# Two projections of a two-block transformer kernel change from full-precision products to rounded high and low parts

## Chip, cores and metric
The kernel runs on one core of one Trainium2 chip. The metric is device time in microseconds (us), from the start of the program to its end. The chip's engines are named as in the profile: PE is TensorE's matmul, PEld its weight load, DVE is VectorE, ACT is ScalarE, POOL is GpSimd, SP the sequencer that issues the transfers (DMA).

## What is computed
The reference runs two blocks over 256 rows of width 1024. The first block has an even and an odd layer of mixed attention; the second has a gated recurrent layer, a latent attention layer and two routed expert layers. The change touches two matrix products:

```
# odd layer of the first block: input projection, 3864 columns wide
p = rms_norm(x, l1_norm) @ l1_w_in
a, b = p[:, 0:512], p[:, 512:1024]            # a * sigmoid(b) goes into a 31-tap convolution
q, k/v, gates, memory q ... = the other columns

# recurrent block of the second
gate_in, rec_in = split(h @ w_in, 2)
gate = gelu(gate_in)
xc = causal 4-tap convolution of rec_in
r, i = sigmoid(xb @ wa + ba), sigmoid(xb @ wx + bx)
a = exp(-8 * r * softplus(-lam));  b = sqrt(1 - a*a) * (i * xc)
hs = associative_scan(a, b)
y = (gate * hs) @ w_out                        # output projection, 1024 x 1024
```

All inputs and results are float32.

## The kernel before
The program is a row of stages. In each stage every engine has its own list of instructions, written out by hand in order; an engine works through its list strictly in order, and semaphores (`wait_ge`, `then_inc`) tie the lists together. Weights come in panels of 512 columns (8 slices of 128 rows, 2 MB) into three slots; `load_panels` on SP issues a panel when the one that had the slot three panels earlier is used up (`acc_ready`).

**Two ways of multiplying.** A plain float32 matmul takes the panel as it is (lines 2171 and 2713). Some projections are computed from rounded parts instead (`project_split`, and `project_rows` with line 628): ACT rounds a slice of the weights to fp32r (the high part, line 656), DVE subtracts it from the original (the low part, the "rest", line 683), the source is split in the same way (lines 648 and 674), and PE adds three products: high by high, high by low, low by high.

**Background work on DVE.** `modulation.add(f, dve, 2)` multiplies one 512 KB tile of a modulation matrix by a row (line 358). Its tiles come into a ring of three; `modulation.load` on SP (line 347) issues tile q only when tile q - 3 is used, and each such wait stands in SP's list in front of the next panel's load.

**The odd input stage (`odd_input`).** PE turns the normed rows in eight steps (line 820), ACT and DVE store them scaled as `HT` (lines 797 and 808), and PE multiplies them with eight panels, two groups of 128 rows each; group j of panel j // 2 is copied out by ACT (line 2189). Between groups `beside(j)` puts small work on PE: after group 4 the product `a * sigmoid(b)` (line 2306) is turned (line 2094) for the convolution, after group 8 the raw keys and values are turned (line 2103), after group 11 come the compression matmuls (line 2114), and after group 15 the finished convolution is turned (line 2157). DVE's list is: its half of `HT`, 14 modulation tiles, the product, convolution taps 0 to 13 (lines 2282 and 2284), the operands of the compression (line 2317, waits for the turned raw rows), taps 14 to 16, sums of squares, taps 17 and 18, norms and rotary turns, taps 19 to 30 with more norms between them, and last the copy of the turned convolution (line 2391).

**The recurrent stage (`lru_block`).** DVE computes the states in two halves of four slices each; `hs_done` counts a half that is multiplied with its gate (line 2834). PE multiplies half 0 with both output panels, then half 1 (line 2713). Meanwhile DVE copies the gate row, runs 8 modulation tiles and the gains, and then scales and adds the four result groups (`gated`, `x_res`, lines 2876 and 2877). Then the rows are normed for the next stage, while PE runs the dummy matmuls of `keep_streaming` (line 317).

Of the kernel before, what the change touches and what calls it, by code (L numbers as in the profile page):

```python
# [97 lines left out]
def build(nc, I, out, upto=99):  # L98
# [1929 lines left out]
    load_early.append((cgain[:, :], bcast(I["l1_c_norm"])))  # L2028
    DQT = zone("d_q_t", [P, D_HEADS, S])
# [11 lines left out]
    cmp_mark = zone.at  # L2041
    RT = zone("cmp_raw_t", [P, 2, D_GROUPS, S])
    OPN = D_GROUPS * N_CMP
    OPS = zone("cmp_operand", [P, 2 * CMP_K * OPN + P - OPN])
    OP = OPS[:, 0:2 * CMP_K * OPN].rearrange("p (i k g n) -> p i k g n", i=2, k=CMP_K, g=D_GROUPS)
    RAW2 = zone("cmp_raw_twice", [P, NT, 2, D_GROUPS, 2, HD])
    room = zone("square_room", [P, 1536])
    K_SLC, K_WIN, M_Q = 2304, 2560, 3352
    dq = lambda h: DQT[:, 2 * (h % 4) + h // 4, :]

    def odd_input():
# [19 lines left out]
        turned_act, turned_dve, _, turn_ahead, turn_behind = turned_rows(odd_rows, [(HT, C("l1_norm", 0, 8), None)])  # L2071
# [5 lines left out]
        with StageBlock() as block:  # L2077
            @block.sync
            def _(sp):
                issue_early(sp)  # L2080
                modulation.load(sp, 28)
                for p in range(ps[0], ps[-1] + 1):
                    load_panels(sp, p + 3)
# [4 lines left out]
            def _(pe):  # L2088
# [72 lines left out]
                for i, p in enumerate(ps):  # L2161
                    n = ODD_PANELS[i][1]
                    w = slots[p % 3][:, 0:KD * n].rearrange("p (k n) -> p k n", k=KD)
                    wait_panel(pe, p)
                    for t in range(NT):
                        j = 2 * i + t
                        wait_acc_free(pe, group(j))
                        for k in range(KD):
                            if j == 0:
                                turn_ahead(pe, k)  # L2170
                            last = nc.tensor.matmul(acc_bank(group(j))[:, 0:n], HT[:, k, t * P:(t + 1) * P], w[:, k, :],
                                                    start=(k == 0), stop=(k == KD - 1))
                            if j == 0:
                                turn_behind(pe, k)
# [4 lines left out]
            def _(act):  # L2179
# [24 lines left out]
                turned_act(act)  # L2204
                evac(0, 1, 2, 3, 4)
# [5 lines left out]
                evac(5)  # L2211
# [37 lines left out]
                evac(14)  # L2249
                for t in range(NT):  # L2250
# [17 lines left out]
            def _(dve):  # L2268
# [52 lines left out]
                conv(14, 17)  # L2321
                dve.wait_ge(squared[0], 3)
# [71 lines left out]
            def _(pool):  # L2394
# [6 lines left out]
                for T in (DQT[:, :, :], MQT[:, :, :], PC[:, :, :, :]):  # L2401
                    f(nc.gpsimd.memset(T, 0.0))
# [4 lines left out]
                                          base=CMP_STRIDE - 1, pattern=[[CMP_STRIDE, D_HEADS]], channel_multiplier=-1), cleared_d)  # L2407

# [195 lines left out]
    LP = CONV_WIDTH - 1  # L2604
    RC = zone("rec_in_t", [P, KD, LP + S])
    GT = zone("gate_t", [P, KD, S])
    XC = zone("conv_t", [P, KD, S])
    R = zone("r_t", [P, KD, S])
    IG = zone("i_t", [P, KD, S])
# [10 lines left out]
    ONES = zone("ones", [P, P])  # L2620

    def lru_block():
# [16 lines left out]
        halves = [slice(0, KD // 2), slice(KD // 2, KD)]  # L2639
        x_done = [sem(f"lru_x_done{x}") for x in range(4)]  # L2640
# [5 lines left out]
        with StageBlock() as block:  # L2646
# [18 lines left out]
            def _(pe):  # L2665
# [37 lines left out]
                for n, half in enumerate(halves):  # L2703
                    for i in range(2):
                        w = slots[outs[i] % 3][:, 0:KD * 512].rearrange("p (k n) -> p k n", k=KD)
                        for t in range(NT):
                            g = gout + 2 * i + t
                            if n == 0:
                                wait_panel(pe, outs[i])
                                wait_acc_free(pe, g)  # L2710
                            pe.wait_ge(hs_done, n + 1)
                            for k in range(half.start, half.stop):
                                last = nc.tensor.matmul(acc_bank(g)[:, :], HS[:, k, t * P:(t + 1) * P], w[:, k, :],
                                                        start=(k == 0), stop=(k == KD - 1), skip_group_check=True)
                            if n:
                                last.then_inc(acc_ready, 1)
# [3 lines left out]
            def _(act):  # L2720
# [27 lines left out]

                turned_act(act)
# [27 lines left out]
            def _(dve):  # L2777
# [47 lines left out]

                def states(n):
# [3 lines left out]
                    for b in range(h.start, h.stop):  # L2830
                        f(v.tensor_tensor_scan(HS[:, b, :], A[:, b, :], TH[:, b, :], 0.0, ALU.mult, ALU.add),
                          wait=(b == h.stop - 1))
                    dve.wait_ge(acc_free["a"], evacuated("gel", 2 * n + 1))
                    v.tensor_tensor(HS[:, h, :], HS[:, h, :], GT[:, h, :], ALU.mult).then_inc(hs_done, 1)
# [24 lines left out]
                states(0)  # L2859
                decays(1)  # L2860
# [1260 lines left out]
```

## Time and profile before
| | |
|---|---|
| median of 3 runs | 2406.74 us (2406.36 to 2407.39) |
| profiled execution | 2404.57 us, its span 2403.3 us |
| PE busy | 2332.0 us, 97% |
| DVE busy | 1856.4 us, 77% |
| ACT busy | 1147.0 us, 48% |
| mean granted TensorE clock | 0.995 |

The span is the time from the first to the last recorded instruction; the rest of the profiled execution lies around it. Times in the rows are us from the span's start. A plain float32 matmul appears as two records. Overlapping records are normal, since the duration of one includes its way through the engine, so the pace of a stream is read from the distance of the starts.

### The profile page before, as it was taken

How to read it: one execution, taken by the hardware profiler on the slowest of the kernel's cores; microseconds unless marked ns; L12 is line 12 of the kernel's file. 1: busy time of each engine (PE TensorE's matmuls, PEld its weight loads, DVE VectorE, ACT ScalarE, POOL GpSimd, SP SyncE). 2: the span in 40 equal slices, each digit the busy share in tenths (PEclk: the TensorE clock that was granted, in tenths of full speed). 3: DMA queues.
4: the chain of work that ended last, by engine and by line, in shares of the span. 5: the costliest groups of instructions: out<-in, count | busy, mean ns of one | idle time of the engine just before them, and what ended most of it. 6: DMA issues, size and time to landing. Idle time of an engine off the chain costs nothing. (4 is left out here: it accounts for less than half of the span.)

```text
span 2403.3 us, 36868 instructions
## 1 busy us (share of the span) xinstructions
PE 2332.0 (97%) x11673; PEld 1907.2 (79%) x11673; DVE 1856.4 (77%) x4221; ACT 1147.0 (48%) x1992; POOL 177.7 (7%) x204
## 2 busy tenths in 40 slices
PE   7989999999999999999999999999999999999997
PEld 5766467868887888888888867788788888888886
DVE  5677776778997788888888855699877777777776
ACT  5674247332485544444444436317744444444443
POOL 1000000001470000000000000026400000000000
PEclk9999999999999999999999999999999999999999
DMA  6534641572214666776676641411255555555553
GB/s 250 195 113 148 239 165 36 194 270 80 91 42 165 246 254 247 258 257 249 251 258 251 253 172 71 149 52 55 90 193 190 192 192 192 192 191 187 190 189 134
DMA packets 144610, 429.28 MB, mean 179 GB/s; under 512 B 15230, under 2 KB 21374, under 8 KB 144510
## 3 DMA queue, kind: packets, MB, share of 16 engines
q1 hardware_dynamic: 144510, 428.08, 49.7%
q8 instruction: 46, 0.75, 0.1%
q14 instruction: 54, 0.44, 0.1%
HBM read 426.99 MB, written 1.05 MB: 178 GB/s over the span
## 5 line engine op out<-in xcount | busy, mean ns | idle before, releaser
L3500 PE MATMUL bank<-v_parts,weighted_high 128*128 128x512 f32 x1936 | 524.3, 392 | 0.5 <-DVE weighted_low L3646 0.5
L3486 PE MATMUL bank<-h_t_parts,u_t_high 128*128 128x512 f32 x1792 | 442.7, 389 | 0.4 <-DVE u_t_low L3621 0.4
L3500 PEld LDWEIGHTS bank<-v_parts,weighted_high 128*128 128x128 f32 x1936 | 348.1, 189 | 65.6 <-issue 2.6
L3486 PEld LDWEIGHTS bank<-h_t_parts,u_t_high 128*128 128x128 f32 x1792 | 336.3, 188 | 70.7 <-DVE u_t_low L3621 0.9
L3568 ACT ACTIVATE u_t_high<-u_ring 128x1024 fp32r<-128x1024 f32 x224 | 237.2, 1059 | 171.7 <-DMA u_ring<-in_peer_u 167.8
L3587 ACT ACTIVATE activated<-activated 128x256 f32<-128x256 f32 x224 | 93.7, 418 | 466.0 <-DVE activated L3634 466.0
L3621 DVE TENSOR_TENSOR u_t_low<-u_ring,u_t_high 128x1024 fp32r<-128x1024 f32 x224 | 273.8, 1222 | 41.2 <-ACT u_t_high L3568 33.9
L3500 PE MATMUL bank<-v_parts,weighted_low 128*128 128x512 f32 x968 | 299.0, 390 | 0.0
L3628 DVE TENSOR_TENSOR v_parts<-v_ring,v_parts 128x1024 fp32r<-128x1024 f32 x240 | 291.9, 1216 | 4.0 <-ACT v_parts L3575 4.0
L3575 ACT ACTIVATE v_parts<-v_ring 128x1024 fp32r<-128x1024 f32 x240 | 253.1, 1054 | 63.5 <-PE bank L3500 62.6
L3489 PEld LDWEIGHTS bank<-h_t_parts,u_t_low 128*128 128x128 f32 x1792 | 244.5, 190 | 17.5
L3489 PE MATMUL bank<-h_t_parts,u_t_low 128*128 128x256 f32 x1792 | 249.9, 282 | 0.0
L3634 DVE TENSOR_REDUCE activated<-bank 128x256 f32<-128x512 f32 x224 | 154.3, 689 | 83.1 <-PE bank L3489 82.2
L3500 PEld LDWEIGHTS bank<-v_parts,weighted_low 128*128 128x128 f32 x968 | 181.7, 188 | 39.7
L3644 DVE CAST weighted_high<-activated 128x256 fp32r<-128x256 f32 x242 | 71.3, 295 | 125.7 <-PE bank L3500 124.0
L3640 DVE TENSOR_TENSOR activated<-activated,gates 128x256 f32<-128x256 f32 x256 | 107.2, 419 | 10.7 <-ACT activated L3580 9.3
L3646 DVE TENSOR_TENSOR weighted_low<-activated,weighted_high 128x256 fp32r<-128x256 f32 x242 | 103.1, 426 | 8.3
L3297 POOL TENSOR_SCALAR onehot<-iota_row,slot_e,slot_gate 128x128 f32<-128x128 f32 x128 | 101.1, 791 | 52.5 <-PE bank_pair L3312 30.8
L3610 POOL TENSOR_TENSOR x_res<-x_res,gated_sum 128x512 f32<-128x512 f32 x2 | 3.3, 1641 | 1344.0 <-DVE gated_sum L3685 1344.0
L3339 ACT ACTIVATE onehot<-onehot,slot_gate 128x128 f32<-128x128 f32 x256 | 87.4, 392 | 0.1
L3273 DVE TENSOR_TENSOR onehot<-bank,slot_e 128x512 f32<-128x512 f32 x128 | 87.2, 681 | 0.0
L3656 DVE SCALAR_TENSOR_TENSOR late_tiles<-late_tiles,bank_pair 128x1024 f32<-128x1024 f32 x70 | 85.0, 1214 | 0.0
(601 smaller groups left out, 3476.5 us busy)
## 6 DMA issues: line engine op xcount, KB each, us to landing
v_ring<-in_peer_v SPq DMA_DIRECT2D x242, 512.0 KB, 3.2
u_ring<-in_peer_u SPq DMA_DIRECT2D x224, 512.0 KB, 4.5
panel<-in_l_w_in SPq DMA_DIRECT2D x15, 2048.0 KB, 8.1
late_tiles<-in_ada_w SPq DMA_DIRECT2D x54, 512.0 KB, 4.2
mod_ring<-in_ada_w SPq DMA_DIRECT2D x42, 512.0 KB, 4.6
panel<-in_peer_w_q SPq DMA_DIRECT2D x8, 2048.0 KB, 7.8
early_u<-in_peer_u SPq DMA_DIRECT2D x22, 512.0 KB, 3.3
panel<-in_l_w_out SPq DMA_DIRECT2D x4, 2560.0 KB, 8.8
```

Source lines behind the costliest of these rows:

```text
L3297: nc.gpsimd.tensor_scalar(O1[:, n % R4, POOL_TOKEN, :], iota[:, :], slot_e1[:, tok], slot_g[:, tok], ALU.is_equal, ALU.mult).then_inc(pool ...
L3486: nc.tensor.matmul(banks[2 + k][:, :], UTH[:, k, j, :], H2[:, j, :, :].rearrange("p a s -> p (a s)"), start=(j == 0), stop=False, skip_gro ...
L3489: last = nc.tensor.matmul(banks[2 + k][:, 0:S], UTL[:, k, j, :], H2[:, j, 0, :], start=False, stop=(j == KD - 1), skip_group_check=True)
L3500: last = nc.tensor.matmul(banks[4 + 2 * t + half][:, :], w[:, t * P:(t + 1) * P], v[k][:, half * 512:(half + 1) * 512], start=opens and n ...
L3568: nc.scalar.activation(UTH[:, s, :, :].rearrange("p a b -> p (a b)"), UR[:, s, :], ACT.Copy)\
L3575: nc.scalar.activation(VH[s], slot, ACT.Copy).then_inc(v_high, 1)
L3587: nc.scalar.activation(AA[:, s, :], AA[:, s, :], ACT.Gelu).then_inc(gelued, 1)
L3621: nc.vector.tensor_tensor(UTL[:, s, :, :].rearrange("p a b -> p (a b)"), UR[:, s, :], UTH[:, s, :, :].rearrange("p a b -> p (a b)").bitcas ...
L3628: nc.vector.tensor_tensor(VL[s], v_slot(b, s)[0], VH[s].bitcast(F32), ALU.subtract)\
L3634: nc.vector.tensor_reduce(AA[:, s, :], banks[2 + s][:, :].rearrange("p (a s) -> p s a", a=2), AX.X, ALU.add).then_inc(summed, 1)
L3640: nc.vector.tensor_tensor(AA[:, s, :], AA[:, s, :], g, ALU.mult).then_inc(w_full, 1)
L3646: nc.vector.tensor_tensor(low[:, :], AA[:, s, :], high[:, :].bitcast(F32), ALU.subtract)\
```

## The change
In `odd_input` the first three of eight panels, and in `lru_block` the whole output projection, are multiplied from rounded parts: ACT writes the high part into a ring (4 slices in the one place, 11 in the other), DVE writes the rest in place over the panel. In `odd_input` the source is split as well (`SRC_HIGH`, `SRC_LOW`) and still stored whole as `HT` for the other five panels. The 14 modulation tiles, which DVE had in a row, are spread: 2 within the first panel, 5 within the second, 1 within the third, 4 behind taps 0 to 13 of the convolution, 2 behind taps 14 to 16; SP's loads follow (`tiles_ahead`). The turning of `a * sigmoid(b)` moves from behind group 4 to behind slice 2 of the third panel. The clearing of `DQT` on POOL waits for the third panel. In `lru_block` the 8 last modulation tiles are put between the last 8 slices' rests.

```diff
@@ odd_input, SP
-                modulation.load(sp, 28)
+                tiles_ahead = {ps[0]: 6, ps[1]: 8, ps[3]: 4, ps[4]: 10}
                 for p in range(ps[0], ps[-1] + 1):
+                    modulation.load(sp, tiles_ahead.get(p, 0))
                     load_panels(sp, p + 3)
@@ odd_input, PE
+                for i in range(SPLIT):                       # SPLIT = 3
+                    wait_acc_free(pe, group(2 * i)); wait_acc_free(pe, group(2 * i + 1))
+                    for k in range(KD):
+                        if i == 0:
+                            pe.wait_ge(src_low, k + 1)
+                        pe.wait_ge(w_low, i * KD + k + 1)
+                        high, low = high_of(i, k), slice_in(LOW_SLOTS, i, k)
+                        for t in range(NT):
+                            for x, (lhs, w) in enumerate(((SRC_HIGH, high), (SRC_HIGH, low), (SRC_LOW, high))):
+                                last = nc.tensor.matmul(...)
+                        ...
+                        if i == 0 and k + 3 < KD:
+                            turn(k + 3)
+                        if i == 2 and k == 2:
+                            beside(4)
@@ odd_input, ACT
+                for k in range(KD):
+                    act.wait_ge(rows_turned, k + 1)
+                    nc.scalar.activation(SRC_HIGH[:, k, :], turned_bank(k), ACT.Copy, scale=norm_gain(k)).then_inc(src_high, 1)
+                    if k % 2:
+                        nc.scalar.activation(HT[:, k, :], turned_bank(k), ACT.Copy, scale=norm_gain(k)).then_inc(plain_act, 1)
+                    round_w(0, k, k + 1)
+                round_w(1, 0, 4)
+                evac(0, 1)
+                round_w(1, 4, KD)
+                round_w(2, 0, 4)
+                evac(2, 3)
+                round_w(2, 4, KD - 1)
...
+                round_w(2, KD - 1, KD)
+                evac(4, 5)
@@ odd_input, DVE
-                turned_dve(dve)
-                modulation.add(f, dve, 28)
+                for k in range(KD):
+                    ... SRC_LOW[:, k, :], and HT[:, k, :] for even k
+                    lower_w(0, k)
+                    if k in (3, 6):
+                        modulation.add(f, dve, 2)
+                for k in range(KD):
+                    lower_w(1, k)
+                    if k < 5:
+                        modulation.add(f, dve, 2)
+                for k in range(4):
+                    lower_w(2, k)
                 ... a * sigmoid(b)
+                for k in range(4, KD):
+                    lower_w(2, k)
+                    if k == 5:
+                        modulation.add(f, dve, 2)
                 dve.wait_ge(conv_in, NT)
                 conv(0, 14)
+                modulation.add(f, dve, 8)
                 ... operands
                 conv(14, 17)
+                modulation.add(f, dve, 4)
@@ lru_block, ACT
+                round_states(0)
                 gelu(2)
                 root(1)
+                round_w(0, 6)
                 gelu(3)
+                round_w(6, 8)
+                round_states(1)
+                round_w(8, len(slices))
@@ lru_block, DVE
                 mults(1)
+                lower_states(0)
                 modulation.add(f, dve, 4)
                 states(1)
+                lower_w(0, 6)
+                gated_states(1)
+                lower_w(6, 8)
+                lower_states(1)
                 ... gate row copied
-                modulation.add(f, dve, 16)
+                for s in range(8, len(slices)):
+                    lower_w(s, s + 1)
+                    modulation.add(f, dve, 2)
```

`round_w` waits until the slice that had its place in the ring is used; `lower_w` waits for the rounded slice.

## Rows read from the trace of the kernel before

**Rows 1.** Timeline of PE, odd input stage (start, duration, engine, line)

```profile
225.11 1.13 PE L2171 MATMUL bank_pair<-panel,h_t 128*128 128x512 f32 x2
...
253.79 7.03 PE L2171 MATMUL bank_pair<-panel,h_t 128*128 128x512 f32 x16
...
268.40 13.90 PE L2171 MATMUL bank<-panel,h_t 128*128 128x512 f32 x32
...
341.65 1.09 PE L2157 MATMUL bank<-ident,conv_out_t 128*128 128x128 f32 x8
```

**Rows 2.** Timeline of DVE, odd input stage (idle before, releaser in brackets)

```profile
262.47 1.38 DVE L2282 TENSOR_SCALAR conv_out_t<-conv_in_t,cols 128x256 f32<-128x256 f32 x4 [4.86 <-ACT conv_in_t L2209]
263.89 22.17 DVE L2284 SCALAR_TENSOR_TENSOR conv_out_t<-conv_in_t,cols,conv_out_t 128x256 f32<-128x256 f32 x52
291.85 4.21 DVE L2317 TENSOR_TENSOR cmp_operand<-cmp_raw_t,cmp_pos_t 64x240 f32<-64x240 f32 x8 [5.78 <-ACT cmp_raw_t L2224]
...
334.23 5.07 DVE L2284 SCALAR_TENSOR_TENSOR conv_out_t<-conv_in_t,cols,conv_out_t 128x256 f32<-128x256 f32 x12
342.34 1.29 DVE L2391 COPY conv_out<-bank 128x512 f32<-128x512 f32 x2 [3.04 <-PE bank L2157]
```

**Rows 3.** Window: odd input stage (busy of PE, PEld, DVE, ACT, POOL; clock; DMA)

```profile
225.00:342.00 117.00, 116.89 (x372) 60.83 (x373) 89.26 (x217) 32.44 (x60) 3.62 (x7) 1.00 0.62 215
```

**Rows 4.** Timeline of DVE in the recurrent stage

```profile
499.82 1.23 DVE L2829 TENSOR_TENSOR tanh_t<-tanh_t,i_t 128x1024 f32<-128x1024 f32 x1 [0.60 <-ACT tanh_t L2747]
501.08 2.44 DVE L2831 TENSOR_TENSOR_SCAN hs_t<-a_t,tanh_t 128x256 f32<-128x256 f32 x4
506.07 1.23 DVE L2834 TENSOR_TENSOR hs_t<-hs_t,gate_t 128x1024 f32<-128x1024 f32 x1 [2.55 <-ACT gate_t L2728]
507.22 1.28 DVE L2867 COPY gate_row<-bank 128x512 f32<-128x512 f32 x2
...
516.75 1.22 DVE L358 SCALAR_TENSOR_TENSOR mod_ring<-mod_ring,silu_c_row 128x1024 f32<-128x1024 f32 x1 [4.58 <-DMA mod_ring<-in_ada_w]
...
532.91 0.69 DVE L2876 TENSOR_TENSOR gated<-bank_pair,gate_row 128x512 f32<-128x512 f32 x1 [2.02 <-PE bank_pair L2713]
```

**Rows 5.** Timeline of PE from the recurrent output into the next stage

```profile
505.18 7.03 PE L2713 MATMUL bank<-panel,hs_t 128*128 128x512 f32 x16
...
532.64 5.32 PE L317 MATMUL bank<-cols,ident 128*128 128x384 f32 x16
538.42 0.85 PE L820 MATMUL bank<-ident,normed_rows 128*128 128x128 f32 x6 [0.45 <-PEq L118]
```

**Rows 6.** Timeline of PE in an output projection that already uses rounded parts

```profile
418.72 0.61 PE L628 MATMUL bank_pair<-slice_parts,src_high 128*128 128x512 f32 x2
...
419.40 0.61 PE L628 MATMUL bank_pair<-slice_parts,src_high 128*128 128x512 f32 x2
```

**Rows 7.** Groups by line, 300 to 900 us (busy, mean ns | idle before)

```profile
L683 DVE TENSOR_TENSOR slice_parts<-panel,slice_parts 128x512 fp32r<-128x512 f32 x18 | 12.3, 691 | 4.1 <-ACT slice_parts L656 4.0
...
L656 ACT ACTIVATE slice_parts<-panel 128x512 fp32r<-128x512 f32 x18 | 11.2, 628 | 4.7 <-PE bank_pair L628 3.2 <-PE bank L628 1.5
...
L674 DVE TENSOR_TENSOR src_low<-bank,src_high 128x256 fp32r<-128x256 f32 x8 | 3.4, 422 | 1.7 <-ACT src_high L648 1.7
```

**Rows 8.** SP's timeline: a panel's load in the recurrent stage

```profile
505.37 0.38 SPq L283 DMA_DIRECT2D panel<-in_peer_w_q  x1
```

**Rows 9.** The page's line on the panels' loads (KB each, median us to landing)

```profile
panel<-in_l_w_in SPq DMA_DIRECT2D x15, 2048.0 KB, 8.1
```

**Rows 10.** Windows around a gap of PE, same columns (clock third last)

```profile
150.00:152.00 2.00, 0.44 (x2) 0.20 (x2) 1.77 (x11) 1.68 (x7) 0.00 (x0) 1.00 0.88 333
152.00:154.00 2.00, 1.84 (x7) 1.43 (x8) 0.97 (x5) 1.25 (x6) 0.00 (x0) 0.69 0.05 16
154.00:156.00 2.00, 2.00 (x11) 2.00 (x10) 1.42 (x8) 1.25 (x5) 0.00 (x0) 0.50 0.00 0
156.00:158.00 2.00, 1.81 (x12) 1.29 (x10) 1.73 (x12) 1.37 (x6) 0.00 (x0) 0.96 0.00 0
```

More of the change, by code:

```diff
@@ L2041, in build @@
     cmp_mark = zone.at
+    HIGH_RING = [nc.alloc_sbuf_tensor_at(f"odd_w_high{i}", [P, 512], F32R, offset=zone.at + i * 2048) for i in range(2)]
     RT = zone("cmp_raw_t", [P, 2, D_GROUPS, S])
@@ L2620, in build @@
     ONES = zone("ones", [P, P])
+    OUT_HIGH = [zone(f"lru_out_high{i}", [P, 512], F32R) for i in range(11)]
+    OUT_LOW = [nc.alloc_sbuf_tensor_at(f"lru_out_low{i}", [P, SLOT // 4], F32R, offset=o)
+               for i, o in enumerate((PANELS, PANELS + SLOT, WORK_END - SLOT))]
     def lru_block():
@@ L2639, in lru_block, with slice_in @@
         halves = [slice(0, KD // 2), slice(KD // 2, KD)]
+        hs_high, hs_low, w_high, w_low, w_used = (sem(f"lru_{x}") for x in ("hs_high", "hs_low", "w_high", "w_low", "w_used"))
+        slices = [(n, i, k) for n in range(2) for i in range(2) for k in range(halves[n].start, halves[n].stop)]
+        def slice_in(tiles, s):
+            _, i, k = slices[s]
+            return tiles[outs[i] % 3][:, k * 512:(k + 1) * 512]
         x_done = [sem(f"lru_x_done{x}") for x in range(4)]
@@ L2702, in _ @@
                                              start=True, stop=True).then_inc(row_ready, 1)
[L2703 to L2716, printed above, removed]
+                for s, (n, i, k) in enumerate(slices):
+                    if n == 0 and k == 0:
+                        wait_acc_free(pe, gout + 2 * i)
+                        wait_acc_free(pe, gout + 2 * i + 1)
+                    if i == 0 and k == halves[n].start:
+                        pe.wait_ge(hs_low, n + 1)
+                    pe.wait_ge(w_low, s + 1)
+                    high, low = OUT_HIGH[s % 11][:, :], slice_in(OUT_LOW, s)
+                    for t in range(NT):
+                        for x, (lhs, w) in enumerate(((HS_HIGH, high), (HS_HIGH, low), (HS_LOW, high))):
+                            last = nc.tensor.matmul(acc_bank(gout + 2 * i + t)[:, :], lhs[:, k, t * P:(t + 1) * P], w,
+                                                    start=(k == 0 and x == 0), stop=(k == KD - 1 and x == 2),
+                                                    skip_group_check=True)
+                        if k == KD - 1:
+                            last.then_inc(acc_ready, 1)
+                    if k < KD - 1:
+                        last.then_inc(w_used, 1)
                 keep_streaming(banks[7], 8)
@@ L2747, in root, with round_w, round_states @@
                     nc.scalar.activation(TH[:, halves[n], :], TH[:, halves[n], :], ACT.Sqrt, scale=-1.0).then_inc(root_ready, 1)
+                def round_w(lo, hi):
+                    for s in range(lo, hi):
+                        wait_panel(act, outs[slices[s][1]])
+                        if s >= 11:
+                            act.wait_ge(w_used, s - 10)
+                        nc.scalar.activation(OUT_HIGH[s % 11][:, :], slice_in(slots, s), ACT.Copy).then_inc(w_high, 1)
+                def round_states(n):
+                    act.wait_ge(hs_done, n + 1)
+                    nc.scalar.activation(HS_HIGH[:, halves[n], :], HS[:, halves[n], :], ACT.Copy).then_inc(hs_high, 1)
                 turned_act(act)
@@ L2859, in _ @@
                 states(0)
+                gated_states(0)
                 decays(1)
```

94 lines of the change are left out of this document (82 added, 12 removed).

## The prediction
> **What bounds the kernel now.** I read the page first: PE is busy for 97% of the span, and the changed places are two short stretches of it. A share over the whole span says nothing about them, so I went to the timelines by engine and looked for the wait that ends last in each.
>
> In the odd input stage PE runs without a pause from 225.11 to 341.65 us. DVE waits twice for PE's results (4.86 and 5.78 us), but from 291.85 to 339.30 (the last taps) it has no idle time; PE reaches the turn of the convolution only 2.35 us after that [rows 1, 2]. So PE is the bound, with DVE close behind: 89.26 us busy of 117, of which the last 47.5 are solid [rows 2, 3]. The reader is to see that DVE's spare time lies in front of 291.85, and that nothing added behind it is free beyond 2.35 us.
>
> In the recurrent output PE runs from 505.18 to 532.64, then DVE scales and adds the last group, norms the rows, and PE turns them from 538.42. DVE works off three of the four groups under PE's matmuls and only one behind them [rows 4, 5].
>
> **PE's side of the sum.** One plain group is 8 slices; two groups with one panel took 268.40 - 253.79 - 0.88 (the turn of the product between the two) = 13.73 us, so a slice for one group costs 0.858 us. With parts three products start within 0.68 us (418.72 to 419.40), 0.227 each [rows 1, 6]. The first three panels are 48 such slices: 41.2 us become 32.7, 8.5 less. The recurrent output is 32: 27.5 become 21.8, 5.7 less. A further sentence of working by rule only: the Trainium skill (TensorE: Matmul & The Clock Gate, Back-to-back issue gap) gives the columns over 2.4 GHz plus 2.5 ns, an estimate of 0.216 us for 512 columns; by it the 240 products would save 2.6 us more. The row of this kernel has 0.227 at full clock, and I use that.
>
> **What is added.** DVE: 24 rests at 0.69 us, which at a stream's overlap of some 0.04 come every 0.65, so 15.6 us, and 8 source rests at 0.42, 3.4 us [rows 7]. ACT gets 24 roundings of 0.63; it is busy 32.44 of 117 us, so it is no bound [rows 3, 7]. The whole source (`HT`) costs as before. POOL's late clearing of `DQT` lies tens of us before its use: nothing.
>
> **Odd stage, step by step.** (1) Start. The first product needs turn, source high, source rest, slice high and slice rest in a row, 0.42 and 0.69 of them on DVE and 0.63 on ACT, in place of one copy: I take +1.7 us (not under 1.1, the two DVE steps; not over the whole 1.74), so PE starts at 226.8. (2) First panel: 8 slices of 1.36 and five turns of some 0.24 give 12.1, its end is 239.0, where half of the old one was left. DVE needs about 1.3 a slice and keeps up. (3) Second panel: each of five slices has a rest (0.65) and a modulation tile (1.22 and a gap, 1.26), 1.91 against PE's 1.36, so DVE is the pace and PE has done slice 4 at 247.5.
>
> (4) Here is the step that I think decides. SP's order is tile 3, 4, 5 (counted in this stage), a panel, then tile 6. Tile 5 goes when tile 2 is used, at 239.6, and the panel right behind it at 240.0. DVE wants tile 6 at 246.1. In the recurrent stage the same order is on record: a panel issued at 505.37, tiles behind it, and DVE stands 4.58 us for one until 516.75, that is 11.4 us after the panel's issue [rows 4, 8]. A panel alone lands in 8.1 [rows 9]. So tile 6 lands between 248.1 and 251.4; I take 250.5, near the row with the same order. Tile 6 then ends at 251.8, the rest of slice 5, queued behind it on DVE, at 252.5, and PE has stood for 5.0 us. Before, DVE waited for tiles as well, but nobody waited for DVE. The Trainium skill (DMA: Bandwidth & Descriptors, Queues, rings and completion order) says that each transfer engine starts descriptors in ring order but that completion is not first in, first out; were the tile free of the panel by that, the wait would go, which is the second rival below.
>
> (5) Gap and clock. With PE busy for 0.44 of 2 us, the granted clock fell to its 1.2 GHz level; over the next three windows it was 0.69, 0.50 and 0.96, which loses 0.62 + 1.00 + 0.08 = 1.7 us of PE's time [rows 10]. A gap of 5 us should do the same: +1.7, between 0 and twice that. (6) Three slices (4.1) and the clock end the second panel at 258.3. The third takes 10.9, the turn 0.9 and some 0.5 for the product, since ACT must copy out two groups behind a table load: 270.6, 2.2 us later than 268.40. (7) The convolution starts when the last rest of the third panel is made, one rounding and one rest after slice 3 is used: 258.3 + 5.5 + 1.4 + 1.7 = 266.9, 4.4 later than before. Taps 0 to 13 take 23.6 (262.47 to 286.06), to 290.5.
>
> (8) Now the moved tiles: four cost 5.0 and, since the fourth is issued only when the first of them is used, some 1.5 of waiting: 297.0. The turned raw rows are there at 270.6 + 23.4 = 294.0, so the 5.78 us of idle time that DVE had is used up, and the operands start 5.2 us later than 291.85. Two more tiles behind tap 16 add 2.5. The solid stretch ends 7.7 us later, at 347.0, while PE is at the turn at 343.9. **DVE has become the bound, and the stage ends 5.4 us later** (1.3 if tile 6 lands at 248.1 and the clock holds; 8 if it lands at 251.4 and the clock loses two such stretches). SP's waits for these tiles also delay two panels, the compression weights and the seventh. Both are wanted behind three further plain panels of 13.73 us each or later, so I cost them at nothing; without that cover it would be up to 8.1. PE's idle time of 3 us before the turn can let the clock fall in the attention: half of 1.7, +0.8.
>
> **Recurrent output, step by step.** DVE: the rest of half 0 takes 1.23 (shape 128x1024), of which 0.60 was idle time; the states start at 500.5 and end at 504.2. Six rests (3.9) bring it to 508.1, the gating 1.2, two rests 1.3, the half's rest 1.2, the gate row 1.3: 513.1. Then eight times a rest and a tile, 1.91 each: 528.4, the gains 0.3, and four groups of scaling and adding, 4 x 1.45 = 5.8: 534.5. Before, the end of that was 532.91 + 1.42 = 534.3 [rows 4, 7]. PE needs 21.8 us from 505.2 but is paced by the rests of the last slices, the last at 527.2, so it ends at 528.5, 4.1 earlier. That is given back whole: three groups that lay under the matmuls now lie behind. Result +0.2. And the dummy matmuls (5.3 us) end at 533.8 while the turned rows need DVE's end plus the same 4.1 us, 538.6: PE is idle for 4.8 us where it was for 0.45 [rows 5], and one more drop of the clock costs 1.7.
>
> **Sum.** +5.4 + 0.8 + 0.2 + 1.7 = +8.1 us on the profiled execution's 2404.57 us (its span is 1.3 less), so 2412.7. The runs' median is 2.2 higher, and on that scale the forecast is 2414.8 us.
>
> **Rivals.** A, the waits come but the clock holds (gaps split up by single slices speak for it): +3.7 and +0.2, so 2410.6. B, tile 6 is on time: PE leaves the second panel at 252.3, the conv starts 1.7 earlier than before, and the tiles behind it bring the solid stretch to 340.4, the turn 1.2 earlier; with +0.2 and between none and one drop of the clock this gives 2406 to 2408. Against it stands the 4.58 us wait; for it, that other panels land faster. C, faster: DVE does not become the bound, and PE's saving reaches the end. Place: DVE's list from 262 on. It needs DVE at the operands before the raw rows are turned, in both stages a pace of the rests under 1.36 us a slice, and no wait for tiles; then 8.5 - 1.7 + 4.1 = 10.9 less, 2396. For it speaks that DVE had 27.7 us idle in the stage; against it that its busy time grows by 19.0 with much of the idle time behind waits that stay. It decides if conv taps start before 259.
>
> **Numbers.** The forecast with both stalls and at least one clock drop 0.43; A 0.20; B 0.22; C 0.12; 0.03 for worse than 2421. What a measurement of this kernel can tell is 0.2%, 4.8 us: below 2401.9 is faster, above 2411.6 slower. A falls a quarter on the slower side (0.05), B wholly within, and C is the faster one: faster 0.12, same 0.15 + 0.22 = 0.37, slower 0.43 + 0.05 + 0.03 = 0.51. The range that leaves out C's far end and the worst is 2403 to 2420.
>
> **What would show it.** DVE waiting for a modulation tile's transfer between the fifth and sixth rest of the second panel, and PE with it; the first tap later than 262.5; no idle time of DVE before the operands; PE idle before it turns the convolution; three results of the recurrent output scaled after PE's last matmul; a clock of 0.50 near 250 and 540 us. The forecast is wrong if tile 6 lands before 247, or if DVE's rests overlap more than the rows of the existing stage show.

## The result, and the profile after

The changed kernel takes 2412.98 us (median of 9 runs) where the kernel before takes 2405.31 in the same runs; the ratio is 1.0031, with a 95% interval of 1.0022 to 1.0041. That is 7.7 us slower, where the sum said +8.1 on the profiled execution. The forecast itself was 2414.8, counted from a median of 2406.74 for the kernel before; from the 2405.31 of these runs the same sum gives 2413.4. In one execution, the one that was profiled first, PE was slowed down from end to end (8299.02 us), so the lines below are from a second set of runs of the same kernel: 2413.41 us against 2404.89, ratio 1.0035 (1.0023 to 1.0047). Its own profiled execution took 2416.38 us (span 2414.9), 3.0 more than its median; where these 3 us lie is said behind the experiments.

The page of the changed kernel, busy time of each engine: PE has lost 4.8 us and DVE gained 29.0, and yet the span has grown.

```profile
span 2414.9 us, 37174 instructions
PE 2327.2 (96%) x11753; PEld 1928.3 (80%) x11753; DVE 1885.4 (78%) x4271; ACT 1177.4 (49%) x2042; POOL 178.1 (7%) x204
```

In the changed kernel the odd stage's products from parts are line 2204, its rests 2379, the taps 2354 and 2356, the turn of the convolution 2179. DVE's timeline in the odd stage (idle time before and its releaser in brackets), which answers to [rows 2]:

```profile
250.72 1.23 DVE L358 SCALAR_TENSOR_TENSOR mod_ring<-mod_ring,silu_c_row 128x1024 f32<-128x1024 f32 x1 [4.12 <-DMA mod_ring<-in_ada_w]
...
251.99 2.49 DVE L2379 TENSOR_TENSOR odd_w_low<-panel,odd_w_high 128x512 fp32r<-128x512 f32 x4
...
266.91 1.38 DVE L2354 TENSOR_SCALAR conv_out_t<-conv_in_t,cols 128x256 f32<-128x256 f32 x4
...
295.32 1.23 DVE L358 SCALAR_TENSOR_TENSOR mod_ring<-mod_ring,silu_c_row 128x1024 f32<-128x1024 f32 x1 [1.15 <-DMA mod_ring<-in_ada_w]
...
296.59 4.20 DVE L2417 TENSOR_TENSOR cmp_operand<-cmp_raw_t,cmp_pos_t 64x240 f32<-64x240 f32 x8
...
342.05 5.07 DVE L2356 SCALAR_TENSOR_TENSOR conv_out_t<-conv_in_t,cols,conv_out_t 128x256 f32<-128x256 f32 x12
```

PE's timeline in the same stage, which answers to [rows 1]:

```profile
225.91 0.77 PE L2204 MATMUL bank_pair<-odd_w_high,odd_src_high 128*128 128x512 f32 x1 [1.73 <-DVE odd_w_low L2379]
...
252.73 0.61 PE L2204 MATMUL bank<-odd_w_high,odd_src_high 128*128 128x512 f32 x1 [4.41 <-DVE odd_w_low L2379]
...
347.18 1.09 PE L2179 MATMUL bank<-ident,conv_out_t 128*128 128x128 f32 x8 [2.86 <-DVE conv_out_t L2356]
349.46 2.90 PE L2536 MATMUL bank<-k_cmp_t,d_q_t 128*128 128x128 f32 x12 [1.20 <-PEq L118]
```

SP's timeline: the panel, and the tiles issued behind it (from 242.16 on):

```profile
240.66 0.43 SPq L283 DMA_DIRECT2D panel<-in_l_w_in  x1
242.16 10.15 SPq L347 DMA_DIRECT2D mod_ring<-in_ada_w  x4
```

The windows of [rows 3] and [rows 10] for the changed kernel (clock third last):

```profile
225.00:342.00 117.00, 110.98 (x409) 70.10 (x410) 101.70 (x236) 47.20 (x88) 3.36 (x6) 0.97 0.62 214
...
248.00:250.00 2.00, 0.32 (x2) 0.00 (x0) 0.00 (x0) 0.63 (x1) 0.00 (x0) 1.00 1.06 426
250.00:252.00 2.00, 0.00 (x0) 0.00 (x0) 1.24 (x3) 0.00 (x0) 0.00 (x0) 1.00 1.02 416
252.00:254.00 2.00, 1.27 (x4) 0.97 (x4) 2.00 (x4) 0.00 (x0) 0.00 (x0) 0.74 0.63 203
254.00:256.00 2.00, 2.00 (x6) 1.61 (x5) 0.48 (x1) 0.48 (x1) 0.00 (x0) 0.50 0.29 119
256.00:258.00 2.00, 2.00 (x9) 1.60 (x9) 0.69 (x1) 0.77 (x2) 0.00 (x0) 0.90 0.00 0
```

The reader is to see one chain. DVE stands 4.12 us for the tile that SP issued behind a panel, PE stands 4.41 us for the rest queued behind that tile, the clock then falls from its 2.4 to its 1.2 GHz level (0.74, 0.50, 0.90: 1.7 us of PE's time), the taps start 4.4 us later than 262.47, the operands start without any idle time, and now PE waits 2.86 us for the last taps, where before it arrived after them. The attention starts at 349.46, where it started at 343.94 before; the 1.20 us pause between the turn and it is the same in both.

The recurrent output. Timeline of DVE, which answers to [rows 4] (line 2964 the rests, 3033 and 3034 the scaling and adding):

```profile
523.18 0.68 DVE L2964 TENSOR_TENSOR lru_out_low<-panel,lru_out_high 128x512 fp32r<-128x512 f32 x1
523.78 1.22 DVE L358 SCALAR_TENSOR_TENSOR mod_ring<-mod_ring,silu_c_row 128x1024 f32<-128x1024 f32 x1
...
537.06 1.22 DVE L358 SCALAR_TENSOR_TENSOR mod_ring<-mod_ring,silu_c_row 128x1024 f32<-128x1024 f32 x1
...
538.62 0.69 DVE L3033 TENSOR_TENSOR gated<-bank,gate_row 128x512 f32<-128x512 f32 x1
...
543.69 0.69 DVE L3034 TENSOR_TENSOR x_res<-gated,x_res 128x512 f32<-128x512 f32 x1
```

And of PE, which answers to [rows 5]:

```profile
470.74 8.86 PE L2787 MATMUL bank<-h_t,panel 128*128 128x256 f32 x32 [2.24 <-DMA panel<-in_lru_w_in]
...
538.69 5.32 PE L317 MATMUL bank<-cols,ident 128*128 128x384 f32 x16
548.47 1.51 PE L820 MATMUL bank<-ident,normed_rows 128*128 128x128 f32 x6 [4.45 <-PEq L118]
```

PE's last product is issued just before 538.69, and all four groups are scaled and added behind it, up to 544.38. PE stands 4.45 us, and the turn then takes 1.51 us in place of 0.85: the clock is at its lower level again.

### The profile page after: what moved, and what is told of

The parts are those of the page before. It is cut to its first block and busy times, and to the rows that moved or that the text cites. A ratio compares the mean times of both kernels' runs of the same rounds, so it can differ in the third digit from the quotient of the medians.

```text
span 8297.6 us, 37174 instructions
## 1 busy us (share of the span) xinstructions
PE 8260.0 (100%) x11753; PEld 4922.2 (59%) x11753; DVE 1898.5 (23%) x4271; ACT 1189.3 (14%) x2042; POOL 178.7 (2%) x204
## 5 line engine op out<-in xcount | busy, mean ns | idle before, releaser
L3657 PE MATMUL bank<-v_parts,weighted_high 128*128 128x512 f32 x1936 | 1729.4, 1099 | 0.0
L3643 PE MATMUL bank<-h_t_parts,u_t_high 128*128 128x512 f32 x1792 | 1534.8, 1096 | 0.0
L3643 PEld LDWEIGHTS bank<-h_t_parts,u_t_high 128*128 128x128 f32 x1792 | 769.2, 429 | 704.8 <-issue 704.8
L3657 PEld LDWEIGHTS bank<-v_parts,weighted_high 128*128 128x128 f32 x1936 | 841.8, 447 | 574.2 <-issue 574.2
L3657 PE MATMUL bank<-v_parts,weighted_low 128*128 128x512 f32 x968 | 925.1, 1093 | 0.0
L3646 PEld LDWEIGHTS bank<-h_t_parts,u_t_low 128*128 128x128 f32 x1792 | 747.5, 459 | 187.1 <-issue 176.8
L3646 PE MATMUL bank<-h_t_parts,u_t_low 128*128 128x256 f32 x1792 | 795.0, 684 | 0.0
L3657 PEld LDWEIGHTS bank<-v_parts,weighted_low 128*128 128x128 f32 x968 | 417.9, 432 | 374.1 <-issue 374.1
L3143 PE MATMUL bank<-h_t,early_u 128*128 128x256 f32 x320 | 263.2, 1103 | 0.0
L3469 PE MATMUL bank_pair<-onehot,onehot 128*128 128x128 f32 x512 | 225.8, 697 | 0.0
```

Source lines behind the costliest of these rows:

```text
L3143: last = nc.tensor.matmul(banks[6 + n % 2][:, 0:S], UE[:, n % 3, k * P:(k + 1) * P], HT[:, k, :], start=(k == 0), stop=(k == KD - 1))
L3469: last = nc.tensor.matmul(banks[s][:, u * P:(u + 1) * P], O2[:, s, u, :], O1[:, s, u, :], start=True, stop=True)
L3643: nc.tensor.matmul(banks[2 + k][:, :], UTH[:, k, j, :], H2[:, j, :, :].rearrange("p a s -> p (a s)"), start=(j == 0), stop=False, skip_gro ...
L3646: last = nc.tensor.matmul(banks[2 + k][:, 0:S], UTL[:, k, j, :], H2[:, j, 0, :], start=False, stop=(j == KD - 1), skip_group_check=True)
L3657: last = nc.tensor.matmul(banks[4 + 2 * t + half][:, :], w[:, t * P:(t + 1) * P], v[k][:, half * 512:(half + 1) * 512], start=opens and n ...
```

## The experiments

Each kernel was timed beside the kernel before on the same chip, in five rounds (three for the two that leave work out). "Difference" is of the two medians, in us.

| kernel | median | before | difference | ratio (95%) |
|---|---|---|---|---|
| changed kernel again | 2413.41 | 2404.89 | +8.52 | 1.0035 (1.0023 to 1.0047) |
| odd part alone | 2410.95 | 2404.89 | +6.06 | 1.0023 (1.0014 to 1.0033) |
| recurrent part alone | 2407.09 | 2404.89 | +2.20 | 1.0009 (1.0000 to 1.0018) |
| changed, tiles in front of the panel | 2408.53 | 2404.89 | +3.64 | 1.0017 (1.0008 to 1.0026) |
| odd alone, late tiles moved out | 2402.76 | 2405.05 | -2.29 | 0.9992 (0.9983 to 1.0001) |
| recurrent alone, no tail tiles | 2401.48 | 2405.05 | -3.57 | 0.9987 (0.9978 to 0.9996) |
| before, no tail tiles | 2404.70 | 2405.05 | -0.35 | 0.9997 (0.9988 to 1.0006) |
| recurrent alone, longer dummy run | 2405.30 | 2405.05 | +0.25 | 0.9999 (0.9990 to 1.0008) |
| odd alone, gap filled | 2410.01 | 2405.06 | +4.95 | 1.0021 (1.0012 to 1.0030) |
| both mended | 2402.36 | 2405.06 | -2.70 | 0.9989 (0.9980 to 0.9998) |
| both, two tiles earlier | 2402.36 | 2405.06 | -2.70 | 0.9988 (0.9979 to 0.9997) |
| the same, shorter dummy run | 2401.06 | 2405.36 | -4.30 | 0.9984 (0.9975 to 0.9993) |

**The changed kernel again, and each part alone.** The three differ in which of the two functions has the change.

> The changed kernel itself, for a trace at full clock. My forecast: +8 us (ratio 1.0034), with VectorE standing some 4.4 us for modulation tile 6 in the second panel, the odd stage ending 5 us later, PE idle 3 us before it turns the convolution, the recurrent stage's result 0.2 us later and PE idle 4.8 us before the next stage. Rival A (no drop of the clock): +4 us. Rival B (tile on time): 0 us. Rival C is out by the first result.

> Rounded parts in the odd input stage alone, the recurrent stage as before. My sum gives the odd part +5.4 and 0.8: +6.2 us, ratio 1.0026. If instead the loss comes from the recurrent stage (VectorE's results behind the matmuls), this kernel is within 2 us of before.

> Rounded parts in the recurrent output alone, the odd stage as before. My sum gives +0.2 and 1.7 for one drop of the clock: +1.9 us, ratio 1.0008. Without the drop of the clock +0.2 us; if PE's 4 us reached the end, -4 us (ratio 0.998).

The odd part costs 6.06 us and the recurrent part 2.20; together 8.26, against 8.52 for both at once. Each interval is some 2 us wide to either side, so this shows no effect of one place on the other and can't exclude a small one; each is studied alone from here on. In the recurrent part alone DVE's last adding ends 103.3 us after the stage's first turn, where the kernel before has 103.7. It is not DVE's end that makes it slower, but what PE does behind it. Timeline of PE, recurrent part alone:

```profile
527.16 5.32 PE L317 MATMUL bank<-cols,ident 128*128 128x384 f32 x16
536.92 1.51 PE L820 MATMUL bank<-ident,normed_rows 128*128 128x128 f32 x6 [4.44 <-PEq L118]
```

Windows of the same kernel (clock third last):

```profile
536.00:538.00 2.00, 1.08 (x5) 1.11 (x6) 0.38 (x1) 0.31 (x1) 0.00 (x0) 0.50 0.13 49
538.00:540.00 2.00, 2.00 (x8) 1.53 (x7) 0.71 (x2) 0.66 (x2) 0.00 (x0) 0.50 0.16 18
540.00:542.00 2.00, 2.00 (x7) 1.43 (x6) 0.54 (x1) 0.47 (x1) 0.00 (x0) 0.50 0.92 283
```

**Is it the tile behind the panel?** The changed kernel, with one more tile issued in front of the first of these panels (the numbers are half tiles), so that the tile of slice 4 is no longer behind the panel:

```diff
-                tiles_ahead = {ps[0]: 6, ps[1]: 8, ps[3]: 4, ps[4]: 10}
+                tiles_ahead = {ps[0]: 8, ps[1]: 6, ps[3]: 4, ps[4]: 10}
```

> The changed kernel with tile 6 issued ahead of the panel instead of behind it (tiles ahead 8 and 6 in place of 6 and 8), the panel so 1.9 us later. My theory: the wait of some 4 us in the second panel and the clock drop with it go, the stage ends 4 to 6 us earlier, total about +2 us (ratio 1.0008 to 1.0015). The rival, that VectorE's plain amount of work sets the end of the stage whatever the order of loads: no change against the changed kernel, +7.5 us.

The wait is gone. DVE's timeline, the last tile of the second panel and the rests behind it:

```profile
245.53 1.22 DVE L358 SCALAR_TENSOR_TENSOR mod_ring<-mod_ring,silu_c_row 128x1024 f32<-128x1024 f32 x1
...
246.79 2.50 DVE L2379 TENSOR_TENSOR odd_w_low<-panel,odd_w_high 128x512 fp32r<-128x512 f32 x4
```

The first tap starts at 260.16 in place of 266.91, and the time falls by 4.88 us, to 3.64 above the kernel before where 2 was expected. PE still stands for DVE at the turn of the convolution:

```profile
340.04 1.97 PE L2179 MATMUL bank<-ident,conv_out_t 128*128 128x128 f32 x8 [2.48 <-DVE conv_out_t L2356]
```

So SP's order made the larger part of the loss, and the tiles put between the taps hold the end of the stage by themselves, here with a lower clock at the turn (1.97 us where 1.09 is the full pace). The tile's wait and the tiles behind the taps are two causes, one behind the other. The trace also says why the time is still above the kernel before, although the turn comes 1.3 us earlier, counted from the stage's first turn: from there to the odd output stage it is 52.17 us where it was 49.64, with turn and attention at the lower clock for a while; PE waits 2.08 us in place of 1.15 for a panel of the recurrent stage, and behind the recurrent output PE stands 4.43 us and its clock falls, after which the rest of the program takes 2.3 us more.

**Take the late tiles out of DVE's solid stretch.** Odd part alone; the four tiles behind tap 13 and the two behind tap 16 go to the odd output stage, and nothing is issued behind the fourth panel:

```diff
-                tiles_ahead = {ps[0]: 6, ps[1]: 8, ps[3]: 4, ps[4]: 10}
+                tiles_ahead = {ps[0]: 8, ps[1]: 6, ps[2]: 2}
...
                 conv(0, 14)
-                modulation.add(f, dve, 8)
...
                 conv(14, 17)
-                modulation.add(f, dve, 4)
...
-                     at_dve={0: dve_gated, 1: dve_mean, 2: dve_scale, 4: dve_conv}, mod_steps=(0, 0), plain=2)
+                     at_dve={0: dve_gated, 1: dve_mean, 2: dve_scale, 4: dve_conv}, mod_steps=(4, 8), plain=2)
```

> Rounded parts in the odd input stage alone, tile 6 issued ahead of the panel, and the six modulation tiles behind the convolution's taps moved to the odd output projection (two in its first panel, four in its second). My theory: VectorE reaches the operands before the raw rows are turned, so PE bounds the stage again and it ends 3 to 4 us earlier than before; the output projection loses 0 to 2 us: 2402 to 2404 us (ratio 0.9985 to 0.9995). The rival, that the 19 us of rests cannot be had on VectorE at all: as the odd part alone with tile 6 on time, 1 to 2 us above before.

This kernel changes DVE's list and SP's order together, so it shows what both do at once. DVE's timeline has its idle time in front of the operands again:

```profile
287.83 4.22 DVE L2416 TENSOR_TENSOR cmp_operand<-cmp_raw_t,cmp_pos_t 64x240 f32<-64x240 f32 x8 [3.94 <-ACT cmp_raw_t L2295]
```

And PE's has none at the turn, so PE is the bound of the stage once more:

```profile
337.63 1.09 PE L2179 MATMUL bank<-ident,conv_out_t 128*128 128x128 f32 x8
339.92 2.25 PE L2534 MATMUL bank<-k_cmp_t,d_q_t 128*128 128x128 f32 x18 [1.20 <-PEq L118]
```

The attention starts 4.02 us earlier than in the kernel before (343.94) and the recurrent stage 3.06 earlier (427.60 against 430.66), but the stage after it only 0.64 earlier (537.78 against 538.42). The 2.4 us between are in the recurrent stage:

```profile
459.59 8.86 PE L2773 MATMUL bank<-h_t,panel 128*128 128x256 f32 x32 [1.89 <-DMA panel<-in_lru_w_in]
```

Before, the same matmuls wait 1.15 us for this panel and take 7.17. A PE that comes earlier waits longer for a transfer, and in this execution its clock fell behind the wait. This profiled execution took 2406.05 us, 3.3 more than the kernel's median (its 11 runs lie between 2401.02 and 2406.88), so the 1.7 us that the lower clock cost in it need not be in the others.

**What hides the gain of the recurrent part?** Two kernels leave out the same eight last modulation tiles, their loads on SP too, and set their results to zero: one with the recurrent part, one without any part of the change.

```diff
@@ recurrent part
-                for s in range(8, len(slices)):
-                    lower_w(s, s + 1)
-                    modulation.add(f, dve, 2)
+                lower_w(8, len(slices))
+                f(v.memset(MOD[:, 34:42], 0.0))
```

> Rounded parts in the recurrent output alone, and the last eight modulation tiles are left out (their eight columns are set to zero, so the second block's second scale is not the reference's). My theory: VectorE's list is what ends this stage; without 10 us of tiles PE is not paced and its saving of 5.7 us arrives, less the eight slices' start: 4 to 6 us below the kernel before without these tiles. The rival, that the plain part of the list (scaling, adding, norm) and PE's own end set it: no difference to the kernel before without these tiles.

> The kernel before with the last eight modulation tiles of the recurrent stage left out (eight columns set to zero). They lay under PE's matmuls, so I expect no change: ratio 1.000, at most 0.5 us less. If they bounded the stage already, 1 us or more less.

Without these tiles the rounded form is 3.22 us faster than the plain one (2401.48 against 2404.70), a little under the 4 to 6 that were expected; with them it is 2.20 slower. Leaving them out of the plain form is worth 0.35, inside its interval. So the tiles and their loads cost nothing under plain matmuls and take the whole gain under the faster ones. The traces divide the 5.4 us between these two cases. Counted from the stage's first turn, PE turns the next rows at 103.79 without the tiles and at 107.34 with them: 3.55 us for DVE's list, which with the tiles ends last (without them DVE waits 2.73 us for PE's products). The rest is the clock: without the tiles PE stands 1.19 us in place of 4.44, and the turn is at full pace (0.85 us).

**Is the rest of it the clock?** Recurrent part alone, with more dummy matmuls, so that PE does not stand before the turn:

```diff
-                keep_streaming(banks[7], 8)
+                keep_streaming(banks[7], 14)
```

> Rounded parts in the recurrent output alone, with 14 instead of 8 dummy matmuls behind them, so that PE stays busy until 0.3 us before it turns the normed rows. If the drop of the clock is what makes this part 2 us slower, it is now level with before (ratio 1.000, +0.2 us). If the loss has another cause, +2 us as without the longer dummy run.

```profile
527.72 9.19 PE L317 MATMUL bank<-cols,ident 128*128 128x384 f32 x28
537.48 0.85 PE L820 MATMUL bank<-ident,normed_rows 128*128 128x128 f32 x6 [0.57 <-PEq L118]
```

The turn is at full pace and the time falls by 1.95 us by the differences, to that of the kernel before. Each of the two differences has an interval of some 2 us to either side, but the traces say the same: from this turn to the end of the span it is 1864.9 us here and in the kernel before, and 1867.6 in the recurrent part alone. The recurrent part's loss is one drop of the clock.

**The same for the odd part's gap.** Odd part alone as in the change, with seven dummy matmuls on PE in front of slice 5 of the second panel; the tile's wait stays.

```diff
+                        if i == 1 and k == 5:
+                            keep_streaming(banks[7], 7)
```

> Rounded parts in the odd stage alone, tile order as changed, but PE runs seven dummy matmuls (4.7 us) where it stood for the tile in the second panel. The wait itself stays. If a drop of the clock behind the gap is part of the loss, as my sum has it, 1.7 us less than the odd part without the filling (2411): 2409 us, and no half clock near 250 us. If the clock has no share: 2411 us.

```profile
246.77 4.68 PE L317 MATMUL bank<-cols,ident 128*128 128x384 f32 x14
251.34 0.50 PE L2206 MATMUL bank<-odd_w_high,odd_src_high 128*128 128x512 f32 x1
...
343.71 1.09 PE L2179 MATMUL bank<-ident,conv_out_t 128*128 128x128 f32 x8 [2.35 <-DVE conv_out_t L2358]
```

Counted from the stage's first turn, the turn of the convolution comes 2.6 us earlier than in the odd part alone (120.3 against 122.95); 0.5 of it is that the tile came earlier in this execution (25.93 against 26.44), and 2.1 is the clock, which stays at 1.00 from 244 to 262. In the two traces 2.4 of the 2.6 us reach the end of the program. By the medians only 1.1 us is left (1.7 was expected), which is inside the intervals; this profiled execution lies 1.5 us below its kernel's median, the other at its own. This run is inconclusive on the time and clear on the mechanism.

**Both parts mended.** First the odd part with its late tiles moved and the recurrent part with 14 dummy matmuls, together.

> Rounded parts in both places, with the odd stage's mends (tile 6 ahead of the panel, six tiles moved to the odd output projection) and 14 dummy matmuls behind the recurrent output. If the parts add: -2.3 us (the odd part so mended) and +0.2 us (the recurrent part with the longer dummy run): 2403 us, ratio 0.9991. If the recurrent part's tail on VectorE still costs something of its own, level with before.

2402.36: the sum of -2.29 and +0.25 is -2.04, measured -2.70. To let the recurrent part gain, DVE's list there must end earlier. So two of its eight tiles go to the odd output stage:

```diff
-                     at_dve={0: dve_gated, 1: dve_mean, 2: dve_scale, 4: dve_conv}, mod_steps=(4, 8), plain=2)
+                     at_dve={0: dve_gated, 1: dve_mean, 2: dve_scale, 4: dve_conv}, mod_steps=(8, 8), plain=2)
...
-                modulation.load(sp, 16)
+                modulation.load(sp, 12)
...
                     lower_w(s, s + 1)
-                    modulation.add(f, dve, 2)
+                    if s < 14:
+                        modulation.add(f, dve, 2)
```

> As the kernel with both mends, but two of the eight tiles in the recurrent stage's tail are done in the odd output projection as well (four in each of its panels). My theory, that VectorE's list ends the recurrent stage: 2 x 1.26 = 2.5 us less there, at most 1 us lost in the output projection, so 1.5 to 2.5 us below the kernel with both mends, 2401 us (ratio 0.998). The rival, that PE's own end bounds it: no difference between the two.

This missed: the time stayed at 2402.36. DVE did end earlier, with the last adding at 530.44, 100.4 us after the stage's first turn (534.13 and 105.2 in the kernel with both mended, whose profiled execution also lost 1.7 us to the clock behind the wait for a panel). DVE's and then PE's timeline say why nothing came of it:

```profile
533.39 0.75 DVE L781 TENSOR_SCALAR normed_rows<-x_res,stats 128x1024 f32<-128x1024 f32 x1
```

```profile
527.50 9.19 PE L317 MATMUL bank<-cols,ident 128*128 128x384 f32 x28
537.14 0.85 PE L820 MATMUL bank<-ident,normed_rows 128*128 128x128 f32 x6 [0.45 <-PEq L118]
```

The normed rows are there at 534.14, but the dummy matmuls run until 536.69. What had been filling was now the bound. It had been so by a little already with all eight tiles: in the recurrent part alone with the longer dummy run the rows are there at 536.42 and the dummy matmuls end at 536.91. And they start 97.4 us after the stage's first turn here and 97.5 there, so moving the tiles did nothing for PE's own end. So the last kernel has two fewer of them:

```diff
-                keep_streaming(banks[7], 14)
+                keep_streaming(banks[7], 12)
```

> The kernel with both parts and two tiles moved earlier, with 12 dummy matmuls of 0.66 us behind the recurrent output in place of 14. Theory (in that kernel DVE's list ended early enough, and PE turned the normed rows late only because its own dummy matmuls still ran): PE turns them 1.3 us earlier than at 537.1, at about 535.8, and the time falls by about that from 2402.4, to 2401. Rival (the end of PE's products, or a drop of the clock in the longer pause, bounds it): no change, 2402.4, or up to 1.7 more if the clock falls to its lower level near 536.

```profile
526.40 7.90 PE L317 MATMUL bank<-cols,ident 128*128 128x384 f32 x24
534.75 0.84 PE L820 MATMUL bank<-ident,normed_rows 128*128 128x128 f32 x6 [0.45 <-PEq L118]
```

Its recurrent stage begins 1.27 us earlier for reasons of its own (428.79 against 430.06); the turn is 2.39 earlier, so 1.12 are from the shorter run. The time is 2401.06 against 2405.36, ratio 0.9984 (0.9975 to 0.9993): the fastest of the whole kernels here, by the differences 12.8 us below the changed one. The dummy run still ends behind DVE (534.30 against 533.02), so about one more of them could go; this was not tried.

## Why the prediction was right, point by point

**Steps 1 to 3.** The first product comes 2.58 us after the stage's first turn, 0.98 before: +1.6 where +1.7 was said. Not foreseen was a stretch at the lower clock in the first panel, behind PE's new 1.73 us wait: products 0.43 us apart in place of 0.23. The odd part alone has the same wait of 1.73 us and no such stretch. The drop was not free: counted from the first turn, SP issues the panel at 17.33 us in place of 15.87, the tile is there at 27.39 in place of 26.44, and the turn of the convolution comes at 123.85 in place of 122.95. The pace of the products is 0.231 us (24 of the recurrent ones in 5.54 us) and not 0.227, so the 240 of them saved 1.0 us less than said; the Trainium skill's estimate of 0.216 in the same place (TensorE: Matmul & The Clock Gate, Back-to-back issue gap) is further off.

**Step 4, the deciding one.** The tile was there at 250.72, said 250.5; DVE waited 4.12 us (4.4) and PE 4.41 (5.0). The tile came 10.1 us after the panel's issue, between the 8.1 of a panel alone and the 11.4 of the earlier row. That the wait hangs on SP's order is shown: with the tiles in front of the panel it is gone. This also bears on the rule weighed there (the Trainium skill, DMA: Bandwidth & Descriptors, Queues, rings and completion order): transfers start in their ring's order, and the trace agrees in so far as a 512 KB tile behind a 2 MB panel did not overtake it.

**Steps 5 to 7.** The clock behind the gap cost 1.7 us, as said (2.1 by the kernel with the gap filled). The second panel ended at 258.57 (258.3), the third at 271.00 (270.6), and the first tap started at 266.91 (266.9).

**Step 8.** The operands started at 296.59 (297.0) without idle time, the solid stretch ended at 347.12 (347.0), PE was at the turn 2.86 us before it, and the attention started 5.5 us later than before (5.4). That the moved tiles hold the end of the stage even without the late tile is shown by the kernel with the tiles in front of the panel, and that they are what held it by the kernel without them between the taps. The panels that SP's waits for these tiles delay were costed at nothing, and PE waits for none of them: its only pause between 271.00 and the attention, other than the 1.20 us, is the 2.86. **The term for the attention was mis-sized**: +0.8 was said, half a drop, and in this profiled execution it lost 2.8 (50.15 us from its start to the odd output stage, 47.35 before), with the clock at its lower level for some 6.8 us behind PE's 2.86 us pause:

```profile
348.00:350.00 2.00, 0.81 (x5) 0.59 (x4) 1.16 (x2) 0.57 (x1) 0.00 (x0) 0.64 1.05 410
350.00:352.00 2.00, 2.00 (x12) 2.00 (x11) 0.00 (x0) 0.71 (x1) 0.00 (x0) 0.50 0.50 195
352.00:354.00 2.00, 2.00 (x11) 2.00 (x11) 0.00 (x0) 0.00 (x0) 0.00 (x0) 0.50 0.01 4
354.00:356.00 2.00, 2.00 (x14) 2.00 (x13) 0.00 (x0) 0.00 (x0) 0.00 (x0) 0.66 0.00 0
```

In the odd part alone the lower level lasts some 3.4 us and the attention loses 1.5 (48.82 us). That trace is at its kernel's median (2410.95 us), so it is the one to add up: the turn of the convolution +5.4 us, counted from the stage's first turn, the attention +1.5, the odd output stage -0.6 (38.81 in place of 39.37), a longer wait for a panel in the recurrent stage +0.8 (1.95 in place of 1.15), the rest of the program -0.4, and -0.4 because the odd stage itself began that much earlier. That is 6.4 between the two spans and 6.06 by the medians, where 5.4 + 0.8 = 6.2 was said. The deciding term was right; that the others, most of which stood in no sum, together come close to the 0.8 that was said is luck. The profiled execution of the whole change, which lies 3.0 us above its median, has more of the same kind than this trace: 0.9 from the first panel, 1.3 in the attention, and some 1.7 behind the wait for a panel.

**The recurrent output.** PE's products were to end 4.1 us earlier and end 4.4 earlier in the recurrent part alone (97.6 us after the stage's first turn, 102.0 before). Three of four groups scaled behind PE's end were said; it was all four, and that is also what the recurrent part alone shows. DVE's end relative to the stage was said at +0.2: -0.4 in that part alone. The profile of the whole change has +2.3 there, of which some 1.7 come from the clock falling behind the 2.24 us wait for a panel at 470.74. PE's idle time was said at 4.8 us and was 4.45, with one drop of the clock: 1.7 said, 1.95 gained back by the longer dummy run. Sum of the part: 1.9 said, 2.20 measured.

**The rivals.** A (waits, but the clock holds) falls, since the clock fell at both places. B (the tile on time) falls as a forecast and is right as a mechanism: put in time, the tile brings 4.9 us back. It had priced the whole at 2406 to 2408, from a median of 2406.74 before; measured was +3.64, which is 2410.4 on that scale. The turn did come 1.3 us earlier than before, counted from the stage's first turn (1.2 said), but behind a 2.48 us wait of PE and at the lower clock, and behind the recurrent output PE stood 4.43 us and its clock fell again; B had counted at most one drop. C needed taps before 259 and no DVE bound. The kernels with the late tiles moved come nearest: their first tap starts at 260.30 at the earliest, and the best of them gets 4.3 of the 10.9 us.

## What to carry to other kernels

A faster matmul is worth only what the next engine leaves: write down when the list of the engine that makes the parts ends, before and after, and move other work out of that stretch first, not into it. Work put between instructions that PE waits for must have its data loaded in front of any large transfer on the same queue, not behind it. Where PE ends earlier than the next rows are ready, resize the dummy run to end with the data it covers: too short loses a clock drop (2.0 us here), too long becomes the bound (1.1 us for two).

## What the runs showed of the hardware

The clock falls in places that nobody touched, and the length of the wait alone does not decide it. The recurrent stage waits for the same panel in each kernel. Behind waits of 0.94 to 1.66 us (eight traces) the matmuls ran at full clock, 7.17 us for 32. Of the five traces with a longer wait, three show the same 32 in 8.86 us (waits of 1.89, 2.08 and 2.24 us) and two in 7.17 (1.95 and 2.08 us). PE's timelines of the changed kernel with the tiles in front of the panel, and of the kernel with both parts mended, have the same wait:

```profile
463.20 7.17 PE L2787 MATMUL bank<-h_t,panel 128*128 128x256 f32 x32 [2.08 <-DMA panel<-in_lru_w_in]
```

```profile
461.15 8.86 PE L2785 MATMUL bank<-h_t,panel 128*128 128x256 f32 x32 [2.08 <-DMA panel<-in_lru_w_in]
```

The first panel of the odd stage shows the same: PE's wait of 1.73 us is the same in all eight kernels with the odd part, and in three of the eight traces (the changed kernel, both mended, two tiles earlier) the clock fell to 0.50 behind it, in the five others it stayed at 1.00. These are single executions, and what decides between them no run here shows. It means that 1 us gained in front of a transfer can be paid with 1.7 behind it: in the profiled execution of the kernel with the late tiles moved, 2.4 of the 3.06 us went there, 0.7 in the longer wait and 1.7 at the lower clock.
